# Norm statistics read straight from PSUM by ScalarE, mixer results gated in PSUM, last chunks tile by tile, and conditioning chunks in pairs

## The reference, cut to what matters

```python
def _rmsnorm(x, w):
    xf = x.astype(jnp.float32)
    y = xf * lax.rsqrt(jnp.mean(xf * xf, axis=-1, keepdims=True) + EPS)
    return (y * w.astype(jnp.float32)).astype(x.dtype)
...
    h = x
    h = h + _hybrid_mixer(_rmsnorm(h, mix_norm_w[l]), ...)
    h = h + _memory_cross_attn(_rmsnorm(h, xattn_norm_w[l]), mem_n, ...)
    h = h + _conv_ffn(_rmsnorm(h, ffn_norm_w[l]), ...)
...
    m = jax.nn.silu(cvec) @ w_mod + b_mod            # 9 x 1024 columns, two layers, x and context
    x = ffn_half_step(x, mx[0:3], ...)               # x + 0.5 * gate * swiglu(rms_norm(x) * (1 + scale) + shift)
...
    o = o / rms(o) * gain * silu(gate)               # at the mixer's end, per head of 64 channels
    return jnp.matmul(o, w_out)
```

## Time and profile before

| | |
|---|---|
| runs, median of 3 | 2205.38 us (2204.9 to 2205.93) |
| profiled execution, device time | 2206.43 us |
| its span of instructions | 2204.6 us |
| TensorE busy | 2116.0 us, 96% |
| VectorE, ScalarE, GpSimd busy | 1004.9, 804.3, 224.7 us |
| chain that ended last | TensorE 86%, VectorE 8%, ScalarE 3%, DMA 1% |
| mean granted clock of TensorE | 0.988 |

### The profile page before, as it was taken

One profiled execution on the slowest core, in us unless ns is written; L12 is line 12 of the kernel. 1 busy time (PEld: TensorE's weight loads), 2 busy tenths in 40 slices (PEclk: granted clock), 3 DMA queues, 4 the chain that ended last, 5 costly groups with the idle time before them and its releaser, 6 DMA issues.

```text
span 2204.6 us, 31783 instructions
## 1 busy us (share of the span) xinstructions
PE 2116.0 (96%) x13881; PEld 1819.7 (83%) x13882; DVE 1004.9 (46%) x1315; ACT 804.3 (36%) x1014; POOL 224.7 (10%) x185
## 2 busy tenths in 40 slices
PE   6988998999999999999999999999999999999997
PEld 6985897999888887788888788888778888868997
DVE  6678554667622332253542232243232235645454
ACT  5642344655532122243332222233222224444443
POOL 1000000303111001100101001111100110001011
PEclk9999999999999999999999999999999999999999
DMA  6425554454641333452343332243234222364552
GB/s 231 146 85 192 192 191 184 149 175 156 217 153 54 128 115 124 175 198 81 132 172 115 124 115 80 79 166 134 103 139 170 74 79 101 115 248 153 173 179 99
DMA packets 53690, 313.96 MB, mean 142 GB/s; under 512 B 5936, under 2 KB 12336, under 8 KB 23728
## 3 DMA queue, kind: packets, MB, share of 16 engines
q1 hardware_dynamic: 51360, 309.51, 39.2%
q10 hardware_dynamic: 2192, 2.43, 0.3%
HBM read 310.86 MB, written 1.05 MB: 141 GB/s over the span
## 4 chain that ended last, share of the span: by engine, by line
PE 86%; DVE 8%; ACT 3%; issue 2%; DMA 1%; SPq 0%; POOL 0%; DVEq 0%; ACTq 0%; POOLq 0%
PE psum L258 26%; PE psum L260 26%; PE psum L259 26%; PE psum L1603 3%; DVE w_lo L242 2%; ACT w_hi L234 1%; PE psum L1259 1%; PE psum L1249 1%; DVE work L410 0%; DVE xn_lo L1776 0%; PE psum L1273 0%; DMA raw<-in_w_in_r 0%; DVE work L1770 0%; DVE work L698 0%; PE psum L874 0%
## 5 line engine op out<-in xcount | busy, mean ns | idle before, releaser
L258 PE MATMUL psum<-xn_hi,w_hi 128*128 128x256 f32 (+1 forms) x2600 | 867.7, 334 | 26.5 <-DVE xn_lo L417 7.4
L259 PE MATMUL psum<-xn_lo,w_hi 128*128 128x256 f32 (+1 forms) x2600 | 855.0, 329 | 0.0
L260 PE MATMUL psum<-xn_hi,w_lo 128*128 128x256 f32 (+1 forms) x2600 | 854.3, 329 | 0.0
L242 DVE TENSOR_TENSOR w_lo<-raw,w_hi 128x2048 fp32r<-128x2048 f32 (+1 forms) x246 | 510.8, 2077 | 414.4 <-ACT w_hi L234 413.5
L258 PEld LDWEIGHTS psum<-xn_hi,w_hi 128*128 128x128 f32 x2600 | 498.8, 192 | 87.2 <-issue 32.2
L259 PEld LDWEIGHTS psum<-xn_lo,w_hi 128*128 128x128 f32 x2600 | 499.2, 192 | 42.5 <-issue 1.0
L260 PEld LDWEIGHTS psum<-xn_hi,w_lo 128*128 128x128 f32 x2600 | 498.7, 192 | 42.5
L234 ACT ACTIVATE w_hi<-raw 128x2048 fp32r<-128x2048 f32 (+1 forms) x246 | 421.7, 1714 | 195.5 <-PE psum L260 167.8
L258 PE MATMUL psum<-h_hi,w_hi 128*128 128x512 f32 (+1 forms) x913 | 315.2, 345 | 1.7 <-POOL h_lo L1578 1.7
L259 PE MATMUL psum<-h_lo,w_hi 128*128 128x512 f32 (+1 forms) x913 | 313.2, 343 | 0.0
L260 PE MATMUL psum<-h_hi,w_lo 128*128 128x512 f32 (+1 forms) x913 | 313.2, 343 | 0.0
(11 more groups left out here) (364 smaller groups left out, 1334.8 us busy)
## 6 DMA issues: line engine op xcount, KB each, us to landing
raw<-in_mod SPq DMA_DIRECT2D x72, 1024.0 KB, 4.8
raw<-in_a_up SPq DMA_DIRECT2D x42, 1024.0 KB, 4.9
raw<-in_b_up SPq DMA_DIRECT2D x42, 1024.0 KB, 4.8
raw<-in_ffn_up SPq DMA_DIRECT2D x22, 1024.0 KB, 5.2
raw<-in_a_down SPq DMA_DIRECT2D x32, 704.0 KB, 4.1
raw<-in_b_down SPq DMA_DIRECT2D x32, 704.0 KB, 4.1
raw<-in_ffn_down SPq DMA_DIRECT2D x16, 704.0 KB, 4.1
raw<-in_wo SPq DMA_DIRECT2D x8, 1024.0 KB, 4.8
```

Source lines behind the costliest of these rows:

```text
L242: dve.tensor_tensor(w_lo[:, slot, 0:size], raw[:, raw_slot(("main", g)), 0:size], w_hi[:, slot, 0:size].bitcast(F32), ALU.subtract).then_i ...
L258: pe.matmul(out, lh, rh, start=first, stop=False, skip_group_check=group)
L259: pe.matmul(out, lh, rl, start=False, stop=False, skip_group_check=group)
L260: return pe.matmul(out, ll, rh, start=False, stop=last, skip_group_check=group)
```

## The change

It does six things.

1. The matrix of ones becomes minus ones (`minus`, `minus_head`). PSUM then holds the negative sum s = -sum(x^2). ScalarE reads it there and looks up the guess r = 1/sqrt(-s/D + eps) by scale and bias (no mean on VectorE ahead of it), and then makes half = r^2 * 0.5/D. VectorE does half = (s - D*eps) * half and r = (half + 1.5) * r: two operations in place of mean and three. `HalfNorm` and three of the mixer's four pairs go the same way. `FinalNorm` and pair 0 keep their mean and lose one step.
2. For pairs 2 and 3 of the mixer the copy L1088 goes. Their squares and their gating read PSUM.
3. The last chunk of the two projections `wo` and `wo2` is done tile by tile (`pe_tile_by_tile`); tile 6 is added and squared beside tile 7's matmuls.
4. For the norms `ffn`, `n25` and `last` ScalarE's table is loaded ahead of the last squares (`early_table`).
5. The output norm (`OutNorm`): ScalarE multiplies by the gain beside the projection, VectorE multiplies by r in two operations of four tiles, and the output is stored by two DMAs, one from SyncE and one from ScalarE.
6. Conditioning chunks go in pairs behind fewer chunks, 12 pairs in place of 24 single ones; behind `wo` stand two in place of three, and the layer's first feed-forward (`a1_up0`) takes three in place of two.

```diff
-    "wo": {3: (3, 2)},
+    "wo": {3: (2, 2)},
     "ffn_down1": {7: (3, 2)},
-    "a1_up0": {c: (1, 1) for c in (1, 3)},
-    "a1_up1": {c: (1, 1) for c in (2, 4, 6, 8)},
-    "a1_down1": {0: (1, 1), 1: (1, 1), 2: (1, 1), 3: (1, 1), 5: (1, 1), 7: (3, 2)},
+    "a1_up0": {2: (2, 1), 5: (1, 1)},
+    "a1_up1": {c: (2, 1) for c in (3, 7)},
+    "a1_down1": {0: (2, 1), 3: (2, 1), 5: (1, 1), 7: (3, 2)},
...
-    "a2_up0": {c: (1, 1) for c in (1, 2, 4, 6, 8, 9)},
+    "a2_up0": {c: (2, 1) for c in (2, 5, 8)},
     "a2_down1": {7: (3, 2)},
-    "b1_up0": {c: (1, 1) for c in (1, 3, 5, 7, 9)},
-    "b1_down0": {c: (1, 1) for c in (0, 2, 4, 6)},
+    "b1_up0": {2: (2, 1), 5: (2, 1), 8: (1, 1)},
+    "b1_down0": {c: (2, 1) for c in (1, 5)},
...
+        def pe_tile_by_tile(pe, s, act_hi, act_lo, n_tiles, k_tiles, k_order):
+            for n in range(n_tiles):
+                for k in k_order:
+                    w = slice((n * k_tiles + k) * P, (n * k_tiles + k + 1) * P)
+                    mm = three_passes(pe, psum[:, s.bank + n, 0:T], (w_hi[:, s.slot, w], w_lo[:, s.slot, w]),
+                                      (act_hi[:, k, X], act_lo[:, k, X]), k == k_order[0], k == k_order[-1])
+                if n == 0:
+                    mm.then_inc(tile_done, 1)
+            return mm
...
+                    if k + self.tiles == KT and self.early_table:
+                        act.activation(col("tables", self.j), col("freq"), ACT.Abs_reciprocal_sqrt)
+                    if self.first_tile is not None and k + self.tiles == KT:
+                        act.wait_ge(tile_added, self.first_tile + 1)
+                        act.activation(nrm[:, k, 0:self.w], xc[:, k, self.span], ACT.Square).then_inc(n_sq, 1)
+                        act.wait_ge(evacuated, s.g + 1)
+                        act.activation(nrm[:, k + 1, 0:self.w], xc[:, k + 1, self.span], ACT.Square).then_inc(n_sq, 1)
...
-                act.activation(col("tables", self.j), col("freq"), ACT.Abs_reciprocal_sqrt)
-                act.wait_ge(n_mean, self.j + 1)
-                act.activation(rstd[:, 0:self.w], mean[:, 0:self.w], ACT.Abs_reciprocal_sqrt).then_inc(n_guess, 1)
+                if not self.early_table:
+                    act.activation(col("tables", self.j), col("freq"), ACT.Abs_reciprocal_sqrt)
+                act.wait_ge(n_sum, self.j + 1)
+                act.activation(rstd[:, 0:self.w], psum[:, 6, 0:self.w], ACT.Abs_reciprocal_sqrt, scale=-1.0 / D, bias=col("eps")).then_inc(n_guess, 1)
+                act.wait_ge(n_guess, self.j + 1)
+                act.activation(half[:, 0:self.w], rstd[:, 0:self.w], ACT.Square, scale=(0.5 / D) ** 0.5).then_inc(n_half, 1)
...
-                dve.tensor_scalar(m, psum[:, 6, 0:self.w], 1.0 / D, EPS, ALU.mult, ALU.add).then_inc(n_mean, 1)
-
-                dve.wait_ge(n_guess, self.j + 1)
-                dve.scalar_tensor_tensor(tmp, r, -0.5, r, ALU.mult, ALU.mult).then_inc(n_rstd, 1)
-                dve.wait_ge(n_rstd, j3 + 1)
-                dve.tensor_tensor(tmp, tmp, m, ALU.mult).then_inc(n_rstd, 1)
-                dve.wait_ge(n_rstd, j3 + 2)
-                dve.scalar_tensor_tensor(r, tmp, 1.5, r, ALU.add, ALU.mult).then_inc(n_rstd, 1)
+                dve.wait_ge(n_half, self.j + 1)
+                dve.scalar_tensor_tensor(t, psum[:, 6, 0:self.w], -D * EPS, t, ALU.add, ALU.mult).then_inc(n_rstd, 1)
+                dve.wait_ge(n_rstd, 2 * self.j + 1)
+                dve.scalar_tensor_tensor(r, t, 1.5, r, ALU.add, ALU.mult).then_inc(n_rstd, 1)
...
-        def gated_dve_copy(dve, o):
-            need(dve, "gat_pe", "out")
-            o(dve.tensor_copy(O4, two_banks(0, T)), "out")
...
+        def mixed(i):
+            return z[:, pair(i), :] if i < 2 else one_bank(i - 2, T)
...
+        class OutNorm(Norm):
+
+            def act_squares_after(self, act):
+                square = super().act_squares_after(act)
+                def evac(s):
+                    square(s)
+                    act.activation(nrm[:, s.c, C], xc[:, s.c, X], ACT.Copy, scale=self.scale(s.c, 0)).then_inc(out_gained, 1)
+                return evac
+            def dve(self, dve):
+                self.dve_stats(dve)
+                for half in range(2):
+                    k = slice(half * KT // 2, (half + 1) * KT // 2)
+                    dve.wait_ge(out_gained, (half + 1) * KT // 2)
+                    dve.tensor_tensor(nrm[:, k, X], nrm[:, k, C], rstd[:, X].unsqueeze(1).to_broadcast([P, KT // 2, T]), ALU.mult).then_inc(out_ready, 1)
...
             post_act_guess(act, 0)
             post_act_guess(act, 1)
             gated_act_out(act)
+            post_act_half(act, 0)
+            post_act_half(act, 1)
             post_act_high(act, 0)
-            need(act, "gat_dve", "out")
+            need(act, "gat_pe", "out")
             act.dma_start(xc[:, :, C], io["ctx"]).then_inc(ctx_in, 16)
             post_act_squares(act, 2)
             post_act_squares(act, 3)
+            post_act_guess(act, 2)
+            post_act_half(act, 2)
             post_act_high(act, 1)
-            post_act_guess(act, 2)
             post_act_guess(act, 3)
+            post_act_half(act, 3)
             post_act_high(act, 2)
             post_act_high(act, 3)
```

More of the change, by code:

```diff
@@ L176, in build @@
         rstd = sb("rstd", [P, 2 * T])
-        mean = sb("mean", [P, 2 * T])
+        half = sb("half", [P, 2 * T])
         mods = sb("mods", [P, 144, 2])
@@ L1792, in evac @@
                     self.dve_add_half(dve, s, gate, 0).then_inc(half_added, 1)
-                    self.dve_mean(dve, 0)
-                    for step in range(3):
+                    for step in range(2):
                         self.dve_newton(dve, 0, step)
@@ L2860 @@
     block("tables", np.zeros((P, 16)))
+    block("eps", np.full((P, 1), EPS))
     head_gain = np.ones((P, 8), np.float32)
```

226 lines of the change are left out of this document (123 added, 103 removed).

## The result

The changed kernel takes 2180.24 us, median of four runs (2177.09 to 2182.45), beside 2205.65 for the kernel before on the same chip: a ratio of 0.9885, with an interval of 0.987 to 0.990. The forecast was 2180.4 and its range 2174.5 to 2189. The total was right; several terms were not, and their errors cancelled. Medians and ratios are of fast runs, so one execution of 2351 us of the kernel before kept busy and one of 4198 us of the kernel before beside it are left out.

The account below looks back on a forecast made before the run. TensorE was taken as the bound nearly everywhere, with idle time, conditioning overhead and low-clock stretches removable. Terms summed to 24.9 us saved: 2181.5 from the profiled 2206.4, median 2180.4, range 2174.5 to 2189.

Parts of the forecast that it names:

- First and memory norm: First two norms: guess and half on ScalarE run beside VectorE's weight splits, saving 1.1 and 1.2 us.
- End of the mixer: Mixer's end: without the copy and with shorter chains, pair 2's low part comes at 225.6, not 230.0; 4.4 us saved.
- Clock behind it: Behind the mixer's end: the shorter wait brings a half-speed stretch taken as half as long; 1.3 us saved (0 to 2.7).
- wo: Behind projection `wo`: TensorE starts at 376.5 instead of 381.3, its first chunk ends 7.0 us earlier (4.8 if clock falls).
- Clock behind wo2: Behind projection `wo2`: the remaining 3.0 us gap still lets the clock fall, for half as long; 0.9 us saved.
- n24: Fourth norm in halves, without cover: 0.9 us for both halves and 0.9 for the clock, 1.8 saved (0.9 to 2.6).
- rival A: Clock still falls behind shorter gaps at mixer's end, `wo`, `wo2`, `n24`: 6.1 us less saved, 2186.5; chance 0.25.
- Pairs: Conditioning chunks in twos: each pair saves 0.24 us, 12 pairs 2.9; the chunk moved to `a1_up0` costs 0.95.
- Output: Output norm and store: last DMA issued at 2198.0 instead of 2199.4, landing at 2202.0; 2.2 us saved (1.0 to 3.0).
- Rival B: Gains at the first two norms and mixer's end absorbed by other queue waits: 6.5 us less saved, 2187; chance 0.12.
- C: Rival: pairs of conditioning chunks hold two of three slots and starve the weights, stalling TensorE: 2210; chance 0.03.
- D: Rival: other waits swallow the chains' gains; only the pairs and the end work, 2.9 + 2.2 us: 2200; chance 0.04.

Follow-up runs that it names:

- the kernel before kept busy: Kernel before plus 22 matmuls that nobody reads in TensorE's 5.2 us wait at the mixer's end: 2202.76 us, ratio 0.9989.
- the profile run again: The changed kernel, unaltered, run and profiled a second time beside the kernel before: 2180.32 us, ratio 0.9889.
- the idle matmuls: The changed kernel plus 11 matmuls that nobody reads in TensorE's wait of 3.7 us behind `wo2`: 2178.33 us, ratio 0.9878.
- the kernel before with the table alone: Kernel before with only the new placing of conditioning chunks, 12 pairs and two chunks instead of three behind `wo`: 2199.14 us, ratio 0.9972.

## Why the prediction was right, point by point

**First and memory norm** (1.1 and 1.2): 1.06 and 1.29. Not tested apart, and the first is known to some 0.4 only: the two other profiles of the kernel before's start stand 0.34 and 0.37 earlier than the first one.

**End of the mixer** (4.4): the walk through both queues was right, 4.33 in the profile run again. In the first profile a low clock under `gated_pe_out` took 1.67 back. The copy alone accounts for 1.28 of it. **Clock behind it** (1.3): mis-sized, 2.4, shown by the kernel before kept busy. The wait that is left, 2.15, brought no fall in seven profiles and one in the eighth.

**wo** (7.0): 6.57, of it 4.63 in TensorE's start (forecast 4.8) and 1.94 by the clock (2.2). **The split of the terms was wrong**, here and at `wo2`. I gave 1.36 to the shorter chain and 0.35 or 0.4 to the tile-by-tile end, and wrote of the earlier sums that they were "worth nothing more". The runs give 1.05 and 1.12 to the tiles and the other 0.56 and 0.55 to the chain. The step that failed: I compared the sums with the end of VectorE's split, but what must be ready by then is the half square, 1.0 us behind the sums. Both together are worth what I said.

**Clock behind wo2** (0.9): -1.1 in the first two profiles, but this is no loss by the change: the kernel before takes 188.9 to 190.3 there and the changed one 189.1 to 190.2. The step that failed is that a shorter wait brings a shorter fall. The wait that is left is 3.68 and not 3.0, since the sums came earlier too, and a low clock followed it in all eight profiles without filling; the idle matmuls show 2.2 at stake. At `n24` (1.8) it varies: 0.8 to 1.5 in the three profiles of the change with a low clock there, and 2.3 in the six without it. Of rival A, half was true.

**Pairs** (2.9, less 0.95 for the moved chunk, so 1.95): 3.35 net in the profile after, 3.5 in the kernel before with the table alone. Mis-sized, 0.44 a pair and not 0.24: the slower first matmuls behind each conditioning chunk weren't in the price.

**Norms in halves** (0.45 each): 0.5, three times. Not tested apart, nor were the earlier table loads.

**Output** (2.2): 2.83. The products took 1.18 each, and the last store landed after 3.4 where I took 4.0. The estimate of 3.2 from the Trainium skill ("DMA: Bandwidth & Descriptors", section on the anatomy of one DMA) was nearer; it lies between the two landings of 3.0 and 3.4.

**Not forecast at all**: 1.63 up to 212 and -1.30 up to 1919.9. The kernel before is at the low clock from 153.6 to 157.0 and the changed one, in work, from 1891.8 to 1898.6. The first accounts for 1.5 of the 1.63: across it the changed kernel's lead grows from 2.3 to 3.8 us. These falls move from profile to profile. Rival B is out (everything upstream was handed on), C and D too.

Of the signs that the prediction named, most came: no wait for `in_mod`, the low part of pair 2 earlier by 4.3 (in the profile run again), a mean clock of 0.991. Three were off: the first chunk behind `wo` takes 6.0 us and not under 6, two conditioning chunks cost 2.12 in a pair and 2.56 apart and not 1.96 and 2.20, and the second store is issued 3.7 ahead of the end and not 4.4.

The sum came out because the errors are of both signs: +1.1 (clock behind the mixer), +0.6 (output), +1.5 (pairs) and +1.6 (up to 212) against -1.7 (mixer's end), -2.0 (clock behind `wo2`), -1.3 (up to 1919.9) and -0.7 (`wo`, `n24`). Five of these eight are the clock's, which no term could have forecast for one profile: that the total came within 0.2 us is luck, that it came within a few is not.

## What to carry to other kernels

A short wait can cost twice where TensorE is the bound: its own length, and a low clock behind it. Matmuls that nobody reads, sized to end 0.3 to 1.2 us ahead of the wait's end, took back the second part at two places, 2.4 and 2.2 us; where TensorE waits again for someone else soon after, they gave nothing. One profile doesn't tell what the clock costs at a place: take several of the same program. When a chain of three engines is shortened, write down when each engine is free and what it needs by then, since two edits that look independent may only pay together.

## What was not expected of the hardware

- The low clock came back at different places in two profiles of one program (209.0 to 212.4 in one, not in the other; 1891.8 to 1898.6 in one, 1892.3 to 1895.8 in the other). The four runs of the change spread over 5.4 us, with mean granted clocks of 0.991 at 2182.2 and 2182.45 and of 0.993 and 0.994 at 2178.25 and 2177.09. A difference of 2 us between single profiles of this kernel proves nothing; a difference over one place does.
- A group of matmuls of 32 weight columns (128*32 in the rows) slows the first full matmuls behind it: 0.34 and then 0.24 from start to start, where it is 0.227 further on.
- A wait of 2.15 us at the mixer's end brought no fall behind it in seven profiles, and one in the run with the copy back; the wait of 2.34 at 183 was followed by one in eleven profiles of fourteen; the wait of 1.56 at `n24` was followed by one in three profiles of the nine that have it. The length of a wait alone doesn't decide; what else does, these runs leave open.
- One of the ten executions of the kernel before kept busy has a mean granted clock of 0.942 and takes 2203.78 us, no longer than others at 0.99. It has no profile, and nothing here explains it.
